# Queries of two heads made tile by tile, gating operands in PSUM, value products and modulation copies moved, in a one-core hybrid decoder step

## The reference

```python
sh1, sc1, g1, sh2, sc2, g2 = jnp.split((jax.nn.silu(c) @ w_ada[l] + b_ada[l])[:, None, :], 6, axis=-1)
h = standardize(x) * (1.0 + sc1) + sh1
parts = jnp.split(h @ w_in[l], PROJ_OFFSETS, axis=-1)
attn, mem, new_state = mixer(*parts)          # block-sparse attention and mLSTM
mixed = jnp.concatenate([attn * beta_attn[l], mem * beta_mlstm[l]], axis=-1)
x = layer_norm(ALPHA * x + g1 * (mixed @ w_out[l]), ln1_g[l], ln1_b[l])
h2 = standardize(x) * (1.0 + sc2) + sh2
f = peer(h2, w_query[l], sub_keys[l], expert_u[l], expert_v[l])
x = layer_norm(ALPHA * x + g2 * f, ln2_g[l], ln2_b[l])
```

```python
idx = jnp.take_along_axis(cand_i, best_j, axis=-1)
act = jax.nn.gelu(jnp.einsum('rd,rpkd->rpk', h, expert_u[idx]))
return jnp.einsum('rpk,rpkd->rd', (softmax(best_s) * act), expert_v[idx])
```

## Time and profile before

| | us |
|---|---|
| median of 3 runs | 1161.06 |
| lowest and highest | 1160.3, 1166.57 |
| the profiled execution's own time | 1167.65 |
| its span | 1165.9 |

### The profile page before, as it was taken

The page is one execution under the profiler, slowest core; times in us unless marked ns, Lnnn a source line. Parts: engine busy times, 40 slices in busy tenths (PEclk is TensorE's granted clock), DMA queues, the critical chain, the costliest instruction groups (busy, mean ns, idle before and its releaser), DMA issues.

```text
span 1165.9 us, 10187 instructions
## 1 busy us (share of the span) xinstructions
PE 904.1 (78%) x2855; PEld 403.4 (35%) x2855; DVE 759.3 (65%) x1645; ACT 192.7 (17%) x571; POOL 624.7 (54%) x605
## 2 busy tenths in 40 slices
PE   3799994487779856598798887777877777777795
PEld 0565641133333345254343432222322222222231
DVE  2277888634517848866666676766786676676635
ACT  0111112271010111111111210210221111021012
POOL 0045567621000004777767677777777777777760
PEclk8899995689769968699999899999999999999998
DMA  9979998779975646999999999999999999999992
GB/s 329 370 263 382 387 394 316 274 278 338 351 277 181 203 172 210 403 410 409 405 409 409 409 409 410 409 409 410 408 411 409 410 409 409 410 409 406 408 368 78
DMA packets 141261, 412.77 MB, mean 354 GB/s; under 512 B 14715, under 2 KB 21632, under 8 KB 138116
## 3 DMA queue, kind: packets, MB, share of 16 engines
q0 software_dynamic: 76608, 278.97, 60.7%
q1 hardware_dynamic: 49492, 109.68, 26.1%
q10 hardware_dynamic: 15106, 23.49, 5.7%
HBM read 405.91 MB, written 6.24 MB: 354 GB/s over the span
## 4 chain that ended last, share of the span: by engine, by line
DMA 33%; POOL 20%; PE 17%; DVE 14%; issue 9%; SPq 6%; ACT 1%; ACTq 0%; DVEq 0%; PEldq 0%; POOLq 0%
POOL ring L533 19%; DMA ring<-in_expert_v,idx 12%; DMA ring<-in_expert_u,idx 10%; PE bank L572 9%; PE bank L575 6%; DMA ring<-in_cache_k 6%; SPq L426 4%; DMA ring<-in_w_ada 3%; DVE ring L1744 3%; SPq L421 2%; DVE ra L1396 1%; PE bank L583 1%; DMA ring<-in_cache_v 1%; DMA ring<-prompt_mods 1%; DVE small L1658 1%
## 5 line engine op out<-in xcount | busy, mean ns | idle before, releaser
L575 PE MATMUL bank<-ring,mix 128*128 128x512 f32 (+1 forms) x1056 | 512.6, 617 | 118.3 <-DMA ring<-in_expert_v,idx 108.4
L1744 DVE CUSTOM_DVE_ANT_0 ring<-ring,bank 128x1024 f32<-128x1024 f32 x256 | 311.0, 1219 | 175.6 <-DMA ring<-in_expert_u,idx 175.1
L575 PEld LDWEIGHTS bank<-ring,mix 128*128 128x128 f32 (+1 forms) x1056 | 183.1, 188 | 435.4 <-DMA ring<-in_expert_v,idx 269.3
L533 POOL DMA_INDIRECT ring<-in_expert_u,idx x264 | 250.1, 947 | 127.9 <-issue 66.8
L533 POOL DMA_INDIRECT ring<-in_expert_v,idx x264 | 250.6, 949 | 90.1 <-issue 62.0
L1292 ACT ACTIVATE mix<-cst,small 128x128 f32<-128x128 f32 (+1 forms) x264 | 92.2, 392 | 254.6 <-PE bank L575 233.2
L490 POOL TENSOR_TENSOR ra<-ra 128x1024 f32<-128x1024 f32 x32 | 75.0, 2345 | 87.4 <-DVE ra L1396 87.4
L478 POOL TENSOR_TENSOR small<-small 128x1 f32<-128x1 f32 (+1 forms) x9 | 6.0, 672 | 173.7 <-DVE small L1661 147.6
L572 PE MATMUL bank<-ht,ring 128*128 128x264 f32 x384 | 93.6, 406 | 3.7 <-DVE w L1386 2.6
L1396 DVE TENSOR_TENSOR ra<-ring,bank 128x2048 f32<-128x2048 f32 x32 | 73.1, 2287 | 34.5 <-PE bank L572 19.7
L572 PE MATMUL bank<-ring,ht 128*128 128x512 f32 (+1 forms) x240 | 82.5, 601 | 2.6 <-ACT ht L1227 1.5
(11 more groups left out here) (314 smaller groups left out, 734.9 us busy)
## 6 DMA issues: line engine op xcount, KB each, us to landing
ring<-in_cache_k SPq DMA_DIRECT2D x128, 256.0 KB, 9.2
ring<-in_cache_v SPq DMA_DIRECT2D x128, 256.0 KB, 4.6
ring<-in_w_ada SPq DMA_DIRECT2D x10, 2048.0 KB, 10.0
ring<-in_w_in ACTq DMA_DIRECT2D x5, 2048.0 KB, 14.8
ring<-in_expert_u,idx POOLq DMA_INDIRECT x264, 13.2
ring<-in_expert_v,idx POOLq DMA_INDIRECT x264, 13.3
ring<-in_w_in SPq DMA_DIRECT2D x2, 2048.0 KB, 20.5
ring<-in_w_ada ACTq DMA_DIRECT2D x2, 2048.0 KB, 10.9
```

The source lines that it names most:

```text
L533: nc.gpsimd.indirect_dma_start(ring_t[:, col(g_in):col(g_in) + DM], None, table, bass.IndirectOffsetOnAxis(tok[:, n * PK + k:n * PK + k + ...
L575: return nc.tensor.matmul(out, lhsT, rhs, start=False, stop=False, skip_group_check=True)
L1744: E.op(v.tensor_tensor_reduce(out=u, in0=u, in1=h2, scale=1.0, scalar=0.0, op0=ALU.mult, op1=ALU.add, accum_out=w[:, k:k + 1]), "u_slot_free")
```

## The change

- The sample gate's `rank`, `am` and `m8` (now `m8p`) lie in PSUM instead of SBUF.
- `ada(7)` goes behind the logits of tile 0, and the V product that stood there goes; of the V products two remain at t = 1, four in chunk 0, two in chunk 1; one stands behind each `mix_T` and six in the sample-state loop. `values_out(0)` goes behind the second chunk.
- The store of the modulation rows (now of all nine rows), the broadcast loads (now into `MOD`) and the loads of ln1 stand in SP's list between the value page loads; the eight sample rows of `MOD` are loaded again after the second normalised tile.
- Both `w_query` blocks that go into the ring are loaded at once after the last V product; the first late one ahead of the ln2 loads.
- The queries of heads 0 and 1 are made for the 128 rows of tile 0 first, then units 0 and 1 are scored; the transpositions of tiles 1 and 2 follow, then the other columns of heads 0 and 1, and heads 2 and 3.
- VectorE runs the top-k of unit 0 between the normalisations of tile 1 and of the sample rows, and that of unit 1 between the products of unit 0.

The diff, cut to its core:

```diff
-        mods = dram("prompt_mods", (1, 6 * DM))
+        mods = dram("mods", (NB + 1, 6 * DM))
...
-        GV = ring[:, 2, 0:3 * DM]
+        GV = MOD[:, 2 * DM:5 * DM]
...
+                if c == 9:
+                    q.wait_ge(sems("ada_out"), 12)
+                    q.dma_start(mods[:, 2 * DM:], MOD[0:NB + 1, 2 * DM:]).then_inc(sems("mods_out"), 16)
+                elif c == 11:
+                    q.wait_ge(sems("mods_out"), 16)
+                    for v, n in enumerate((2, 4, 3)):
+                        load(GV[:, v * DM:(v + 1) * DM], mods[NB:NB + 1, n * DM:(n + 1) * DM].partition_broadcast(P), "ln1_in")
+                elif c == 13:
+                    q.wait_ge(sems("state_T_out"), 1)
+                    load(RA[:, 2 * DM:3 * DM], A["ln1_g"].partition_broadcast(P), "ln1_in")
+                    load(RA[:, 3 * DM:4 * DM], A["ln1_b"].partition_broadcast(P), "ln1_in")
...
-            q.wait_ge(sems("state_T_out"), 1)
-            load(RA[:, 2 * DM:3 * DM], A["ln1_g"].partition_broadcast(P), "ln1_in")
-            load(RA[:, 3 * DM:4 * DM], A["ln1_b"].partition_broadcast(P), "ln1_in")
...
-            q.wait_ge(sems("ada_out"), 12)
-            q.dma_start(mods[0:1, 2 * DM:], MOD[8:9, 2 * DM:]).then_inc(sems("mods_out"), 16)
             q.wait_ge(sems("kv_used"), 2 * KQ)
-            q.wait_ge(sems("mods_out"), 16)
-            for v, n in enumerate((2, 4, 3)):
-                load(GV[:, v * DM:(v + 1) * DM], mods[0:1, n * DM:(n + 1) * DM].partition_broadcast(P), "ln1_in")
...
-            weights(BQ, w_q, 0)
+            for j in range(2):
+                weights(BQ + j, w_q, j)
+            q.wait_ge(sems("h2_ready"), 2)
+            load(MOD[0:NB, 2 * DM:5 * DM], mods[0:NB, 2 * DM:5 * DM], "ln1_in")
             q.wait_ge(sems("h2_ready"), 3)
-            weights(BQ + 1, w_q, 1)
             q.wait_ge(sems("cs_stored"), 32)
+            load(WQ_LATE.rearrange("p (k n) -> p k n", k=KT), w_q[:, :, 2 * N:3 * N], "wq_in")
             load(RA[:, 0:DM], A["ln2_g"].partition_broadcast(P), "ln2_in")
...
-            load(RA[:, 2 * DM:3 * DM], mods[0:1, 5 * DM:6 * DM].partition_broadcast(P), "ln2_in")
-            for j in range(2):
-                if j:
-                    q.wait_ge(sems("wq_used"), 1)
-                load(WQ_LATE.rearrange("p (k n) -> p k n", k=KT), w_q[:, :, (2 + j) * N:(3 + j) * N], "wq_in")
+            load(RA[:, 2 * DM:3 * DM], mods[NB:NB + 1, 5 * DM:6 * DM].partition_broadcast(P), "ln2_in")
+            q.wait_ge(sems("wq_used"), 1)
+            load(WQ_LATE.rearrange("p (k n) -> p k n", k=KT), w_q[:, :, 3 * N:4 * N], "wq_in")
...
-            ada(7)
 
             q.wait_ge(sems("rs_seen"), 1)
...
-                values()
                 if t:
+                    values()
                     ada(9)
                     values()
+                else:
+                    ada(7)
                 E.wait("probs")
...
-                values(2)
+                if c == 0:
+                    values(2)
                 E.wait("chunk_done")
...
             values()
             mix_T(1, 0)
+            values()
             E.wait("state_T_out")
...
-                    if k % 4 == 3 and vh[0] < 16:
+                    if k % 3 == 1 and vh[0] < 16:
                         values()
...
-            for t in range(3):
+            def h2_T(t):
+
...
                 E.op(m, "tail_mm")
-                E.wait("h2T_out")
...
-            def queries(c):
+            def queries(c, to, cols):
...
-                    m = mm(bank[Q_BANK[c]][:, 0:R], w[:, k * N + (c % 4) * P:k * N + (c % 4 + 1) * P], HTv[:, k, :],
+                    m = mm(to[:, cols], w[:, k * N + (c % 4) * P:k * N + (c % 4 + 1) * P], HTv[:, k, cols],
...
+            h2_T(0)
+            q.wait_ge(sems("sk_in"), 16)
+            for e in range(2):
+                m = tr(bank[2][:, e * P:(e + 1) * P], SKN[:, e * P:(e + 1) * P])
+            E.op(m, "tail_mm")
+            E.wait("h2T_out")
+            block_in(BQ)
+            for c in range(4):
+                if c >= 2:
+                    q.wait_ge(sems("q_out"), c - 1)
+                queries(c, bank[4 + c % 2], slice(0, P))
+            E.wait("sk_out")
+            q.wait_ge(sems("q_out"), 2)
+            scores(0)
+            q.wait_ge(sems("q_out"), 4)
+            h2_T(1)
+            scores(1)
+            E.wait("h2T_out")
+            h2_T(2)
+            E.wait("h2T_out")
+            for c in range(8):
+                if c == 4:
+                    block_in(BQ + 1)
+                if c >= 4:
+                    q.wait_ge(sems("q_out"), c + 1)
+                queries(c, bank[Q_BANK[c]], slice(P if c < 4 else 0, R))
+                if c % 4 == 3:
                     used()
...
+            def late_queries(c):
+
+                if c % 4 == 0:
+                    q.wait_ge(sems("wq_in"), 16 * (c // 4 - 1))
+                q.wait_ge(sems("q_out"), c + 3)
+                queries(c, bank[Q_BANK[c]], slice(0, R))
+                if c == 11:
                     E.sync()
                     q.sem_inc(sems("wq_used"), 1)
...
             E.wait("zeros_ready")
...
                     if n + 2 < PH:
-                        q.wait_ge(sems("q_out"), 2 * (n + 3))
+                        q.wait_ge(sems("q_out"), 2 * (n + 5))
                     scores(n + 2)
                 accumulate(n)
...
-                E.op(a.activation(QT[:, h:h + PH + 2:PH + 1, e, :], new[:, 0:SEQ].rearrange("p (t r) -> p t r", t=2), ACT.Copy))
+                if c < 4:
+                    E.op(a.activation(QT[:, h + PH + 1, e, :], new[:, P:2 * P], ACT.Copy))
+                else:
+                    E.op(a.activation(QT[:, h:h + PH + 2:PH + 1, e, :], new[:, 0:SEQ].rearrange("p (t r) -> p t r", t=2), ACT.Copy))
...
+            h2T_out(0)
+            E.wait("tail_mm")
+            E.op(a.activation(SKT, bank[2][:, 0:256], ACT.Copy), "sk_out")
+            for c in range(4):
+                E.wait("tail_mm")
+                E.op(a.activation(QT[:, c // 2, c % 2, :], bank[4 + c % 2][:, 0:P], ACT.Copy), "q_out")
+            h2T_out(1)
+            h2_to_bank(0)
+            best(0)
+            h2T_out(2)
             for c in range(8):
                 query_out(c)
...
-            rank, am, AM, rm = W[:, 192:256], W[:, 256:320], W[:, 320:448], W[:, 1536:1664]
+            AM, rm = W[:, 320:448], W[:, 1536:1664]
+            rank, am, m8p = (bank[2][0:NB, 64 * i:64 * i + c] for i, c in ((1, 64), (2, 64), (3, 8)))
...
-            step(v.tensor_reduce(m8[0:NB, :], rm.rearrange("p (g h) -> p h g", h=AH), AX, ALU.max))
-            step(v.tensor_tensor(m8[0:NB, :], m8[0:NB, :], nl[0:NB, :], ALU.max))
-            E.op(v.tensor_tensor(pn[0:NB, :], nl[0:NB, :], m8[0:NB, :], ALU.subtract))
+            step(v.tensor_reduce(m8p, rm.rearrange("p (g h) -> p h g", h=AH), AX, ALU.max))
...
-                    q.wait_ge(sems("kv_used"), KQ + 16)
-                    values_out(0, None)
                 E.wait("intra")
...
             step(v.tensor_copy(evT, bank[6][:, 0:32]), "ev_out")
+            q.wait_ge(sems("kv_used"), KQ + 16)
+            values_out(0, None)
...
-            for t in range(3):
-                E.wait("y_mm", 1 if t < 2 else 2)
+
+            def norm2(t):
+
+                E.wait("y_mm")
...
-                    if 0 < n < LAST and k < TOPK_PARTS:
+                    if n < LAST and k < TOPK_PARTS:
                         topk(n + 1, k)
...
-            for n in range(2):
-                for part in range(TOPK_PARTS):
-                    topk(n, part)
+            norm2(0)
+            norm2(1)
+            E.wait("y_mm")
+            for part in range(TOPK_PARTS):
+                topk(0, part)
+            q.wait_ge(sems("ln1_in"), 96)
+            norm2(2)
+            E.op(v.memset(MIX[0:NB, 2048:2560], 0.0), "zeros_ready")
             for n in range(UNITS):
                 dots(n)
```

37 lines of the change are left out of this document (6 added, 31 removed).

## The result

The changed kernel takes 1158.89 us (median), the kernel before 1164.51 beside it: ratio 0.9948, 95% interval 0.9934 to 0.9963. The gain is real and small: 6 us where 26 were forecast.

What follows compares the result with a forecast made beforehand. The prediction took the expert stage's gather stream (DMA full, 409 GB/s) as the bound: 14.4 us ahead of the normalisations plus 12.3 behind, less 0.7, gives 26 us, from the 1161.06 median to 1135.0; range 1124 to 1153.

Steps and rivals of the forecast that it cites:

- Gate: Sample gate: operands in PSUM end four VectorE stalls, some 12.5 us, but ada(6) is next, so 3.2 us gained.
- Attention: I take 1 us: Attention stage: ada(7) and a V product moved out of the way gain 1 us (loss of 2 to gain of 5).
- One product fewer is due there: some 3.5 us, with the 1 us above in it: mLSTM chunk 0: one V product fewer before chunk 1, which begins some 3.5 us earlier, attention's 1 us included.
- V products out of chunk 1: Second mLSTM chunk: two V products leave its end, so the steps behind it start at about 309.7, 18.6 us earlier.
- One V product (1.9) is added ahead of the loop: Between the chunks and the sample-state loop: one added V product costs 1.9 us, so the loop starts at 326.
- rival 1: Sample-state loop: value pages come late, it ends at 380 as before; 1147 us in all; chance 0.13.
- Queries of tile 0: Behind the loop: four query pieces at full clock take 8.6 us, top-k of unit 0 runs from 404.1 to 412.7.
- Rival 2: Query part: TensorE's clock falls, four pieces cost 8.6 us more and the stream loses 10; 1153 us; chance 0.09.
- rival 5: Sample-state loop: it runs at half clock because PE idles ahead of it, ending at 409; 1178 us; chance 0.05.
- The first gather is possible 34 us earlier: Expert stage's start: early top-k of unit 0 allows the first gather 34 us earlier.
- Less 0.7 for the stream: Gather stream up to unit 1's products: 20 gathers carried against 20.5 before, so 0.7 us is taken off the gain.
- Rival 4: Whole chain: it waits for chunk 0 and 1 pages anyway, and gathers starve by their early start; 1161 us; chance 0.07.

Runs made afterwards that it cites:

- e4: The changed kernel with the gate's rank, am and m8 back in SBUF; ratio 0.9961 to the kernel before.
- e5: The changed kernel with the modulation blocks of ada(10) and ada(11) one pair of page loads earlier in SP's list; ratio 0.9872 to the kernel before.
- e12: The kernel before with only the move of e5 in SP's list; ratio 1.0002 to the kernel before.
- e1: The changed kernel with GpSimd's two sample-tile roots behind the second and fifth gather of unit 0; ratio 0.9889 to the kernel before.
- e3: The changed kernel with top-k of unit 0 back behind all three normalisations on VectorE; ratio 0.9907 to the kernel before.
- e6: e1 with the ln2_g and ln2_b loads ahead of SP's wait for the third normalised tile; ratio 0.9859 to the kernel before.
- e7: e1 with tile 0's transposition, queries and unit 0's scores ahead of the sample rows' projection; ratio 0.9829 to the kernel before.
- e10: The changed kernel with the two V products behind the second mLSTM chunk put back; ratio 1.0049 to the kernel before.
- e11: The changed kernel with the three broadcast loads of the modulation rows back behind the last V product; ratio 0.9960 to the kernel before.
- e2: The changed kernel with one V product back in tile 0 of the attention, behind ada(8); ratio 0.9926 to the kernel before.

## Why the forecast was wrong

Of the error of 23.9 us in the time (1158.89 - 1135.0), 3.5 are the reference: the median of the kernel before is 1164.51 here, not 1161.06. 4.7 lie in the profiled executions (3.1 above and 1.6 below their medians). 15.4 us are missing at the products of unit 1 (468.10 - 452.7): 8.0 ahead of the first normalisation (381.63 - 373.6), 7.4 behind it. Ahead of it the changed kernel lies behind the forecast by 5.4 us at the start of chunk 1 (293.48 against 288.1), by 5.7 at the steps behind the chunks, by 8.2 at the start of the loop and by 7.8 at its end. So two stretches lost the 8 us, the one up to chunk 1 and the one between the chunks and the loop.

- **Gate.** The operations took the 0.15 to 0.4 us that were forecast, and ada(6) was next, as forecast (213.18). The 3.2 us end at the blocks of ada(10) and ada(11). The sum of the forecast does not hold them either: it takes 1 us for all that happens up to the end of the attention. e4 could not size them, as only three of its stalls came back.
- **"Attention: I take 1 us".** The path was named rightly: the stage ended with ada(11), whose block SP issues behind eight page loads (251.32, 3.6 us earlier than before; forecast 2.4). The size is near, 0.2 us at the start of chunk 0. What I did not ask is what TensorE does with the time that is taken out of its order when the blocks come no earlier: it stands, 7.25 us ahead of ada(10) and 2.50 ahead of ada(11), and what follows has to be paid at a lower clock (next item). e5 moves nothing but the two blocks and gives 8.8 us; e12 shows that the same move is worth nothing where TensorE's own work still covers it.
- **"One product fewer is due there: some 3.5 us, with the 1 us above in it" (the step that failed first).** Chunk 1 began 1.9 us later than before instead of 3.5 earlier. Of these 5.4 us, 0.8 are the attention's.
  - The lower clock, 2.8: the operations of chunk 0 ahead of its first V product took 6.02 us (268.67 to 274.69) instead of 3.23 (268.86 to 272.09). The granted clock was 0.66 to 0.78 from 250 to 280 (before 1.00), so TensorE spent part of this stretch at the lower of its two levels (1.2 GHz), behind the two waits in which it stood. In e5, which waits 1.65 us in their place, the same operations took 3.23 us again (259.35 to 262.58; granted clock 1.00 from 260 to 270).
  - The stretch from there to chunk 1, 1.8: it became 0.7 us shorter instead of 2.5. One product fewer was due, but the product that went was also one that let SP load on, so the waits for pages in chunk 0 hardly fell (3.69 us, before 4.25).
  - Other executions: the traces of e1, e3, e6, e7, e10 and e11 have the same program on TensorE up to there. In them chunk 1 begins between 291.4 and 296.6, never near 288, and the clock shows again: where it was 1.00 from 270 to 280 (e6, e11) chunk 0 lasts 21.2 and 21.4 us, where it was 0.75 to 0.83 (the others and the changed kernel) 23.8 to 25.9.
- **V products out of chunk 1.** Mechanism right: e10 gives it 11.8 us. The forecast for this pair was 11.3: the 18.6 without the 3.5 of the item above, less 3.8 for the pair in the loop. That the size fits so well is luck: between e10 and the changed kernel the steps behind the chunks moved by 12.7 us, not by 15.1, and the loop by 0.7, not by 3.8.
- **"One V product (1.9) is added ahead of the loop".** From the steps behind the chunks to the loop it took 18.8 us instead of 14.3, so the addition cost 4.6, not 1.9. With the product came the clearing of the second accumulation group's banks (2.07 us at 321.89; in the kernel before it lay in chunk 1), and the product itself took 2.77 us (at 331.53; the granted clock was 0.55 from 320 to 330 and 0.83 from 330 to 340).
- **The loop.** 41.6 us against 41.4 forecast; page waits in it were small (0.28 us), so rival 1 (pages late in the loop) did not happen. e2 adds that the last product is hidden by VectorE's last update (TensorE waits 1.97 us there without it), so the price of 1.90 each is not the price of the sixth.
- **Copies.** "No wait at the first normalisation" came true (0.24 us). e11 shows that it is worth nothing that could be measured; by its trace the bytes among the pages cost now about what the wait cost before.
- **Queries of tile 0.** The four pieces took 7.41 us (forecast 8.6), top-k 8.6, the scores came 29.1 us behind the first normalisation (forecast 30.5). Rival 2 and rival 5 did not happen.
- **"The first gather is possible 34 us earlier" (the second step that failed).** It came 18.9 earlier (428.71 against 447.61), although its numbers were ready 27 us earlier. I moved top-k past the sample normalisation on VectorE, and did not follow the move on GpSimd, whose program has that normalisation's roots ahead of the gathers. The trace of before could not show a wait there, as the roots were long done. e1 mends it and gets 6.9 us; e3 shows that without it the early top-k was worth less than nothing. This program order is the reason for most of the 7.4 us.
- **"Less 0.7 for the stream".** The products of unit 0 began at 433.81, 52.2 behind the first normalisation (forecast 50.8), but from there to unit 1's products it took 34.3 us instead of 28.3. The six are VectorE's waits for gathers (6.04 us in five waits from 437 to 453) that started late and shared the DMA engines with 3.7 MB of late loads (DMA share 1.03 from 434 to 460). e1 takes off the first cause, e6 part of the second.

The two mends, e1 and e5, give 6.9 + 8.8 = 15.7 us. That this is about the 15.4 that were missing is in part chance. e1 gives back what the second step lost. e5 does more than give back the first: it brings chunk 0 to 259.35, 8.5 us ahead of where the forecast had it, so part of its gain is one that the forecast never counted. No run undoes the lower clock or the costlier added product by itself; their sizes are read from the traces. "Wrong if the loop ends after 375" was the sign that I had named; it ended at 375.81. The other sign, more than 8 us of idle DMA between the first gather and the products of unit 1, did not come: the DMA share of these 39.4 us was 0.92.

Rival 4 (the freed chain waits for pages, and the gathers starve by what they gain) comes nearest by its number, 1161. Its first half happened in chunk 0, but more of the loss there is the lower clock; the late gathers have another reason, the roots ahead of them. The clock, which rival 2 had fall in the queries, fell in the attention stage.

## What to carry to other kernels

When an operation moves past another on one engine, list what the second one asks of every other engine, and look up where that stands in *their* programs: an order that never showed a wait can become the bound. When work is taken away in front of a load, ask what that load is queued behind; a wait of 0.45 us in the trace of before is no bound on the wait after. When loads are paced by the work that uses them, taking a piece of that work away also takes away the load that it would have let out. And look for the stretches in which DMA moves nothing: a megabyte moved there gave back 3.1 us by the traces (e6), against 2.6 for its bytes at 409 GB/s.

## What the runs showed of the hardware

How many of the gate's operations stall beside GpSimd is not fixed. With the operands in SBUF the kernel before had four (3.04, 3.71, 3.01, 3.66 us); e4, with the same operations, three, in VectorE's timeline:

```profile
200.86 3.03 DVE L1482 TENSOR_SCALAR ra<-ra 8x64 f32<-8x64 f32 x1
203.93 0.26 DVE L1483 COPY ra<-ra 8x128 f32<-8x128 f32 x1
...
204.94 2.73 DVE L1488 TENSOR_TENSOR small<-small 8x8 f32<-8x8 f32 x1
...
207.78 3.87 DVE L1490 TENSOR_TENSOR ra<-ra,small 8x128 f32<-8x128 f32 x1
```

GpSimd's step beside this copy in e4, and then the same copy and step in the kernel before:

```profile
203.93 3.72 POOL L501 TENSOR_TENSOR mod<-r,small 128x2032 f32<-128x2032 f32 x1
```

```profile
205.57 3.71 DVE L1454 COPY ra<-ra 8x128 f32<-8x128 f32 x1
205.57 3.59 POOL L498 TENSOR_TENSOR mod<-r,small 128x2032 f32<-128x2032 f32 x1
```

The copy at 203.93 started in the same hundredth as GpSimd's step and took 0.26 us; in the kernel before the same copy, at 205.57 as GpSimd's step, took 3.71. The stalls end with GpSimd's steps: in e4 the operation at 204.94 ends at 207.67, the step at 207.65. The Trainium skill (SBUF — State Buffer, Who interferes with whom) says that whoever issues first gets the shared pair of ports and the other is blocked for the whole instruction. The ends of the stalls agree with this; which of the two issued first at 203.93 and at 205.57 the traces are too coarse to show, so that the phase of the two engines makes three stalls out of four is likely, not shown.

The forecast weighed another rule of the Trainium skill (SBUF — State Buffer, SBUF: two separate sides), by which two-port operations of VectorE hold up the making of descriptors: up to 1.2 us here. e1 shows gathers beside the sample normalisation: one of six took 1.37 us (425.23), the others 0.94 to 1.06, as without it (e3: 0.93 to 1.06). The cost was some 0.4 us there (which operation of VectorE it waited for is not shown); the second root, between two gathers, took 1.37 us instead of 0.54, and VectorE waited 0.54 for it. e6 and e7, with the same order, show the same times (1.37 and 1.37 to 1.38).
